# Layer 0's value transposes, sample outputs and last gates, layer 1's query norm rounds and tile copies put in other places

## The chip, the cores and the metric

The kernel runs on one core of a Trainium2 chip. The metric is the device time of one execution in microseconds (us). Five engines work side by side and meet at semaphores: TensorE (PE, with its weight loads as PEld), VectorE (DVE), ScalarE (ACT), GpSimd (POOL) and SyncE (SP); the last two issue most of the DMAs.

## What is computed

Two layers of a hybrid decoder, for a prompt of 512 tokens and for 8 samples of one token each, with the same weights. Both go through the same matmuls as 520 columns.

```python
# layer 0: gated linear attention (4 heads) and retention (4 heads), both recurrent
h  = rms_norm(x, norm_g) * (1.0 + scale) + shift          # scale, shift, gate: silu(c) @ w_ada + b_ada
qa, ka, va, ra, ga, qb, kb, vb, gb = split_cols(h @ w_in, EVEN_SIZES)
o_inter   = q_decayed @ state;  o_intra = scores @ v      # by chunks of 64 tokens
new_state = exp(b_last) * state + k_dec.T @ v             # also for each of the 8 samples
o = rms_norm(o, head_norm_g) * silu(g)
x = x + gate * (concat(oa, ob) @ w_out)
# layer 1: stick-breaking attention (8 heads, q and k normed) and a chunked spatial gate (8 groups)
qc, kc, vc, gc, ud, vd, gd = split_cols(h @ w_in, ODD_SIZES)
log_beta = log_sigmoid(z);  log_rest = where(mask, log_sigmoid(-z), 0)
weight   = exp(log_beta + cumsum_from_right(log_rest) - log_rest);  oc = weight @ v
# the samples attend to 2048 cached keys and values, 16 pages of 128 through a page table
od = gelu(ud) * (tril(w_s) @ rms_norm(gelu(vd)) + b_s)
x = x + gate * (concat(oc * silu(gc), od * silu(gd)) @ w_out)
```

## The kernel before

Activations lie with features on partitions (16 chunks of 128) and the 520 tokens along the free axis. fp32 products are made of two parts: each weight tile (1024 columns of `raw`) is split by ScalarE into `w_hi` (`hi`) and by VectorE into the rest `w_lo` (`lo`), and TensorE multiplies hi*hi, hi*lo and lo*hi. One such tile half is a **unit**: 8 chunks of 6 matmuls, 48 in all; two units fill an output tile in one of two PSUM pairs `pt`, which an engine then copies ("evac") to a buffer `G[...]`. `w_hi` and `w_lo` have two places each, so the split of the unit after next can start only when the unit at hand is done.

The phases follow one another: modulation vectors (`ada0`), the gate's low rank (`ra`), layer 0 (`l0`, 8 heads: 4 GLA, 4 retention), its output projection (`out0`), layer 1's queries and gate inputs (`l1a`, 4 rounds of 8 units), layer 1's heads (`l1b`, 8 heads of 10 units) and `out1`.

Around the units each engine runs the same hand-written order of **steps**. Every phase has a generator on every engine (`mix`), and `go_on(mix)` after a unit runs the next step. In a head of `l0` the units are numbered 0 to 27; 12 of them are weight tiles (u = 2, 3, 8, 9, 12, 13, 16, 17, 22, 23, 26, 27) and the others short matmuls for the modulation of later layers. Steps run after each tile unit and after u = 7 and 21. The function `passed` first plays the second half of the previous head (`rest0`, at u = 2 to 16) and then the first half of this head (`first0`, six steps at u = 17, 21, 22, 23, 26, 27). The last head of layer 0 uses `last_passed`, which also plays four steps of its own `rest0` (`own`) inside and after its last units; the others are played among the first units of `out0`.

`first0` before: PE step 2 (u=21) the decay sums (GLA) or the rotation swap (retention), once key and query are evacuated; step 4 (u=23) ten transposes of the values into M[0] to M[2] (`v_t`), after `qk`; step 5 (u=26) key transposes and scores (`sc`); step 6 (u=27) the first four key-value products (`kv`). VectorE copies the samples' values (`srow0`) from M[0], GpSimd sends them to DRAM and back as a broadcast (`vb_in`), and VectorE, after its first four state steps (`state_steps(i, 0)`), adds them to the eight sample states (eight instructions on one line, semaphore `st_step`). `rest0` before: PE step 1 (u=2) the sample outputs (`os`) and the other four `kv`; step 2 (u=3) the prompt's outputs (`o`).

In `l1a`, ScalarE squares a pair of query tiles at step Q_AT, TensorE sums them over partitions with a matmul by ones at Q_AT+1, and VectorE applies the norm at Q_AT+2. A round of `l1a` has nine steps: one before its first unit and one after each of its 8 units; steps 8 and 9, and 17 and 18, follow each other with no unit between.

Of the kernel before, what the change touches and what calls it, by code (L numbers as in the profile page):

```python
# [12 lines left out]
P = 128  # L13
D = 2048
KC = D // P
T = 512
# [48 lines left out]

Q_AT, V_AT = [4, 8, 13, 17], [22, 26, 31, 35]
L1A_STEPS = 36
# [56 lines left out]
def build(nc, a, o, cst):  # L124
    ctx = ExitStack()
    with ctx:
# [391 lines left out]
        def last_passed(rest, first, own):  # L518

            yield  # L520
            for n in range(8):
                if n != 2:
                    go_on(rest)
                yield
            for n in range(6):
                go_on(first)
                yield
            for n in range(4):
                go_on(own)
                yield  # L530

        def passed(rest, first):
# [12 lines left out]
        def _(pe):  # L545
# [143 lines left out]
            def first0(i, gla):  # L689
                yield  # L690
                pe.wait_ge(s("evac"), i * 6 + (T_L0 + 4))
                if isinstance(i, int) and i == 0:
                    pe.wait_ge(s("la_copied"), 2)
                    pe.wait_ge(s("const_in"), 16 * NCONST)
                else:
                    pe.wait_ge(s("mixed"), i * 2)
                if gla:
                    pe.wait_ge(s("lah"), i + 1)
# [9 lines left out]
                yield  # L708
                yield
                pe.wait_ge(s("qk"), i + 1)  # L710
                for t in range(NT):
                    for d in range(2):
                        tr(M[1 + t // 2][:, 256 * (t % 2) + P * d:256 * (t % 2) + P * d + P],
                           G[d][:, P * t:P * t + P])
                tr(M[0][0:NB, 0:P], G[0][:, T:N])
                tr(M[0][0:NB, P:2 * P], G[1][:, T:N]).then_inc(s("v_t"), 1)
                yield

                pe.wait_ge(s("srow0"), i + 1)
                for t in range(NT):  # L720
                    tr(M[0][:, P * t:P * t + P], G[3][:, P * t:P * t + P])
                pe.wait_ge(s("vtok"), i + 1)
                for t in range(NT):
# [18 lines left out]

            def rest0(i):
                pe.wait_ge(s("st_step"), i * 8 + 8)
                pe.wait_ge(s("sct"), i + 1)
# [3 lines left out]
                last.then_inc(s("os"), 1)  # L749
                key_values(i, 1)  # L750
                yield
                pe.wait_ge(s("s_step"), i * 8 + 8)
# [51 lines left out]
            def l1a_mix():  # L804
                for n in range(L1A_STEPS):
                    for r in range(4):
                        if n == Q_AT[r] + 1:
                            pe.wait_ge(s("q_sq"), r + 1)
                            for t in range(2):
                                mm(M[t], ones[:, :], tmp[t][:, 0:T])  # L810
                                last = mm(M[2][:, 8 * t:8 * t + 8], ones[:, :], tmp[t][:, T:N])
                            last.then_inc(s("q_ss"), 1)
                    if n == Q_AT[3] + 4:
                        pe.wait_ge(s("q_col"), 1)
                        tr(M[1][0:64, 0:P], qcol).then_inc(s("q_t"), 1)
# [149 lines left out]
        def _(act):  # L965
# [13 lines left out]

            def walk(name, i, order, mix=None, ahead=(0, 1), fine=()):  # L980

                go_on(mix)
                split = split_ahead(order, ahead)
                for u in range(2 * len(order)):
                    if u in fine:
                        go_on(mix)
                    if u in split:
                        hi(name, i, split[u])
                    if goes_on(name, order, u):
                        go_on(mix)  # L990
# [75 lines left out]
            def first0(i, gla):  # L1066
                if gla:
                    f(lah, la[:, :, bass.ds(i * P, P)], ACT.Copy).then_inc(s("lah"), 1)
                yield
                if gla:  # L1070
# [6 lines left out]
                yield  # L1077
                act.wait_ge(s("v_t"), i + 1)
                f(vtok[:, 0:2, :], M[1].rearrange("p (t d) -> p t d", t=2), ACT.Copy)
                f(vtok[:, 2:4, :], M[2].rearrange("p (t d) -> p t d", t=2), ACT.Copy).then_inc(s("vtok"), 1)  # L1080
                yield
# [105 lines left out]
            def l1a_mix():  # L1187
                for n in range(L1A_STEPS):
                    for r in range(4):
                        if n == Q_AT[r]:  # L1190
                            act.wait_ge(s("evac"), T_L1A + 2 * r + 2)
                            f(pair_a, pair(r), ACT.Square).then_inc(s("q_sq"), 1)
                        if n == Q_AT[r] + 1:
                            act.wait_ge(s("q_ss"), r + 1)
# [6 lines left out]
                        value_gate(r, n - V_AT[r])  # L1201
                    if n == Q_AT[3] + 4:
                        act.wait_ge(s("q_t"), 1)
# [71 lines left out]
            def l1b(i, odd):  # L1275
                mix = mix1(i, odd)
                walk("l1b", i, L1B_ORDER, mix)
                finish(mix)

            l1b(0, 0)  # L1280
            step.straight()
# [47 lines left out]
        def _(dve):  # L1329
# [27 lines left out]
            def walk(name, i, order, evac=None, par0=0, group=None, mods=(), mix=None, ahead=(0, 1), late=None, fine=()):  # L1357
# [11 lines left out]
                for u in range(2 * len(order)):  # L1369
# [7 lines left out]
                    if order[u // 2] is TILE and u % 2 == 1:  # L1377
                        if t not in late:
                            read_out(t, u)
# [137 lines left out]

            def first0(i, gla):
                yield
                yield  # L1520
# [5 lines left out]
                else:  # L1526
# [13 lines left out]
                yield  # L1540
                dve.wait_ge(s("v_t"), i + 1)
                copy(srow0, M[0][0:NB, 0:256]).then_inc(s("srow0"), 1)
                yield
# [3 lines left out]
                    .then_inc(s("sct"), 1)  # L1547
                dve.wait_ge(s("st_in"), i * 16 + 16)
                step(tt(st, st, small[:, 24:32].unsqueeze(2).to_broadcast([P, NB, 256]), ALU.mult))
                yield  # L1550
                state_steps(i, 0)
                dve.wait_ge(s("vb_in"), 16 * 2 * HEADS + 32 if isinstance(i, int) and i == 2 * HEADS - 1
                            else i * 16 + 16)
                for b in range(NB):
                    stt(st[:, b, :], values(i, b), G[3][:, T + b:T + b + 1], st[:, b, :], ALU.mult, ALU.add)\  # L1555
                        .then_inc(s("st_step"), 1)
                yield

# [18 lines left out]
            def rest0(i):  # L1577
# [178 lines left out]
            def l1a_mix():  # L1756
                for n in range(L1A_STEPS):
                    for r in range(4):
                        if n == Q_AT[r] + 2:
                            dve.wait_ge(s("q_rs"), r + 1)  # L1760
# [4 lines left out]
                        value_gate(r, n - V_AT[r])  # L1765
                    if n == Q_AT[3] + 2:
                        copy(qcol.rearrange("p (b h) -> p h b", b=NB), wide[:, 0:HC, T:N]).then_inc(s("q_col"), 1)
# [380 lines left out]
```

## Time and profile before

| what | us |
|---|---|
| median of 3 runs (2292.97 to 2308.41) | 2301.32 |
| the profiled execution | 2311.7 |
| its span, first to last instruction | 2310.2 |
| mean granted TensorE clock, of full speed | 0.956 |
| `ada0` and `ra`, 0 to 162 | 162 |
| `l0`, 162 to about 954 | 792 |
| `out0` and norm, to about 1185 | 231 |
| `l1a` and `l1b`, to about 2084 | 899 |
| `out1`, to the end | 226 |

The stages are read from the chain and the timeline. "Waits" are an engine's idle time before an instruction, put down to what released it. The granted clock is given in shares of full speed: 1.00 is 2.4 GHz and 0.50 is 1.2 GHz, values between are means over a stretch.

### The profile page before, as it was taken

How to read it: one execution, taken by the hardware profiler on the slowest of the kernel's cores; microseconds unless marked ns; L12 is line 12 of the kernel's file. 1: busy time of each engine (PE TensorE's matmuls, PEld its weight loads, DVE VectorE, ACT ScalarE, POOL GpSimd, SP SyncE). 2: the span in 40 equal slices, each digit the busy share in tenths (PEclk: the TensorE clock that was granted, in tenths of full speed). 3: DMA queues.
4: the chain of work that ended last, by engine and by line, in shares of the span. 5: the costliest groups of instructions: out<-in, count | busy, mean ns of one | idle time of the engine just before them, and what ended most of it. 6: DMA issues, size and time to landing. Idle time of an engine off the chain costs nothing.

```text
span 2310.2 us, 45308 instructions
## 1 busy us (share of the span) xinstructions
PE 2146.0 (93%) x16847; PEld 1888.8 (82%) x16847; DVE 1179.9 (51%) x3657; ACT 587.0 (25%) x733; POOL 201.9 (9%) x319
## 2 busy tenths in 40 slices
PE   6889999999999999799979997999999899999997
PEld 2268888888888878699968897888788788888997
DVE  1533434434454454644462377677677677745332
ACT  1322212121221212322232232233223132324221
POOL 0000101101010110100000001111101101100011
PEclk8789999999999999899979998999999999999999
DMA  9876656466665656333332256887877877853441
GB/s 316 299 235 193 206 171 193 157 200 200 183 189 179 188 166 201 103 115 114 109 138 73 84 165 225 289 279 262 294 255 256 279 245 265 285 174 97 135 128 62
DMA packets 401526, 444.99 MB, mean 193 GB/s; under 512 B 17268, under 2 KB 307406, under 8 KB 399807
## 3 DMA queue, kind: packets, MB, share of 16 engines
q1 hardware_dynamic: 359270, 311.99, 43.9%
q0 software_dynamic: 32288, 122.12, 15.4%
q10 hardware_dynamic: 9810, 8.73, 1.1%
q8 instruction: 103, 1.69, 0.3%
q14 instruction: 55, 0.45, 0.1%
HBM read 416.18 MB, written 26.61 MB: 192 GB/s over the span
## 4 chain that ended last, share of the span: by engine, by line
PE 68%; DVE 15%; DMA 6%; issue 5%; ACT 4%; DVEq 0%; SPq 0%; ACTq 0%; POOLq 0%; POOL 0%
PE pt L547 54%; PE m L547 12%; DVE arena L1727 4%; DMA arena<-in_cache_k 4%; ACT w_hi L969 2%; ACT arena L969 2%; PE m L551 2%; DVE w_lo L1341 1%; DMA raw<-in_e_w_ada 1%; DVE arena L1555 1%; DMA arena<-in_o_k_norm_g 1%; DVE arena L1573 1%; PE pt L551 1%; DVE arena L1515 1%; DVE arena L1891 1%
## 5 line engine op out<-in xcount | busy, mean ns | idle before, releaser
L547 PE MATMUL pt<-act_hi,w_hi 128*128 128x260 f32 x4384 | 918.2, 291 | 42.2 <-DVE w_lo L1341 13.3
L547 PE MATMUL pt<-act_hi,w_lo 128*128 128x260 f32 x4384 | 894.7, 286 | 0.0
L547 PE MATMUL pt<-act_lo,w_hi 128*128 128x260 f32 x4384 | 894.4, 286 | 0.0
L547 PEld LDWEIGHTS pt<-act_hi,w_hi 128*128 128x128 f32 x4384 | 690.1, 193 | 107.0 <-issue 91.7
L1341 DVE TENSOR_TENSOR w_lo<-raw,w_hi 128x1024 fp32r<-128x1024 f32 x274 | 335.3, 1224 | 845.4 <-ACT w_hi L969 845.1
L547 PEld LDWEIGHTS pt<-act_lo,w_hi 128*128 128x128 f32 x4384 | 689.9, 192 | 0.0
L547 PEld LDWEIGHTS pt<-act_hi,w_lo 128*128 128x128 f32 x4384 | 688.5, 192 | 0.0
L969 ACT ACTIVATE w_hi<-raw 128x1024 fp32r<-128x1024 f32 x274 | 289.8, 1058 | 1159.9 <-PE pt L547 1143.0
L1727 DVE CUSTOM_DVE_ANT_0 arena<-arena 128x128 f32<-128x128 f32 x1024 | 224.7, 287 | 60.6 <-DMA arena<-in_cache_k 60.3
L969 ACT ACTIVATE arena<-arena 128x1040 f32<-128x1040 f32 (+8 forms) x191 | 158.1, 837 | 230.5 <-DVE arena L1827 83.0
L547 PE MATMUL m<-raw,cond 128*9 128x512 f32 x768 | 133.8, 663 | 16.4 <-DMA raw<-in_e_w_ada 14.1
L547 PE MATMUL m<-arena 128*128 128x256 f32 (+6 forms) x704 | 128.0, 412 | 21.0 <-DVE arena L1555 20.2
L547 PEld LDWEIGHTS m<-arena 128*128 128x128 f32 (+4 forms) x704 | 79.2, 175 | 60.2 <-DVE arena L1555 21.9
L1976 POOL DMA_DIRECT2D arena<-in_cache_k x128 | 68.0, 531 | 624.7 <-DVE arena L1727 310.6
L547 PEld LDWEIGHTS m<-raw,cond 128*9 128x9 f32 x768 | 17.1, 91 | 81.5 <-DMA raw<-in_e_w_ada 42.9
L551 PE MATMUL m<-c_ident,arena 128*128 128x128 f32 (+2 forms) x403 | 58.3, 276 | 26.0 <-DMA c_fold<-const_fold 8.8
L547 PEld LDWEIGHTS m<-arena,ones 128*128 128x128 f32 (+1 forms) x236 | 43.6, 204 | 43.1 <-issue 19.0
L547 PE MATMUL m<-arena,ones 128*128 128x512 f32 (+3 forms) x236 | 65.5, 392 | 14.4 <-ACT arena L969 8.4
L969 ACT ACTIVATE arena<-m 128x512 f32<-128x512 f32 (+2 forms) x93 | 49.9, 573 | 96.1 <-PE m L547 73.8
L551 PEld LDWEIGHTS m<-c_ident,arena 128*128 128x128 f32 (+2 forms) x403 | 45.0, 143 | 28.6 <-DMA c_fold<-const_fold 8.8
L547 PE MATMUL m<-arena,mod 128*8 128x256 f32 x1024 | 67.2, 380 | 0.0
L2047 POOL TENSOR_SCALAR arena<-arena 128x256 f32<-128x256 f32 x56 | 53.3, 952 | 135.6 <-DVE arena L1566 77.6
(169 smaller groups left out, 1147.3 us busy)
## 6 DMA issues: line engine op xcount, KB each, us to landing
arena<-in_cache_k POOLq DMA_DIRECT2D x128, 512.0 KB, 5.2
arena<-in_cache_v SPq DMA_DIRECT2D x128, 512.0 KB, 5.4
raw<-in_o_w_in SPq DMA_DIRECT2D x112, 512.0 KB, 6.2
raw<-in_e_w_in SPq DMA_DIRECT2D x98, 512.0 KB, 4.6
raw<-in_e_w_ada SPq DMA_DIRECT2D x96, 512.0 KB, 5.8
raw<-in_o_w_ada SPq DMA_DIRECT2D x96, 512.0 KB, 5.2
raw<-in_e_w_out SPq DMA_DIRECT2D x32, 512.0 KB, 3.9
raw<-in_o_w_out SPq DMA_DIRECT2D x32, 512.0 KB, 4.8
```

Source lines behind the costliest of these rows:

```text
L547: return pe.matmul(out, lhsT, rhs, start=start, stop=stop, skip_group_check=True)
L551: return pe.transpose(out, x, ident[0:k, 0:k])
L969: return act.activation(out, x, fn, **kw)
L1341: tt(w_lo[:, b, :], raw[:, sl, :], w_hi[:, b, :].bitcast(F32), ALU.subtract)\
L1515: return ts_(d, x, SCALE, None, ALU.mult) if to == 2 else copy(d, x)
L1555: stt(st[:, b, :], values(i, b), G[3][:, T + b:T + b + 1], st[:, b, :], ALU.mult, ALU.add)\
L1573: stt(S[:, n % 2, :], S[:, (n - 1) % 2, :], small[:, at + 2:at + 3], tmp[4][:, 0:256], ALU.mult, ALU.add).then_inc(s("s_step"), 1)
L1727: last = dve.tensor_tensor_reduce(kpage, kpage, qb[:, P * h:P * h + P], 1.0, 0.0, ALU.mult, ALU.add, to[:, 8 * p + h:8 * p + h + 1])
L1891: tt(z, z, m012[:, 0:SB_ALL], ALU.subtract).then_inc(s("lw"), 1)
L1976: pool.dma_start(pages[:, key_slot(p), :], ck[bass.ds(page, 1)].rearrange("n s d -> (n s) d"))\
L2047: pool.tensor_scalar(carry[:, n, :], S[:, (n - 1) % 2, :], small[:, 6 * (n // 2) + n % 2:6 * (n // 2) + n % 2 + 1], None, ALU.mult).then_i ...
```

## The change

- Layer 0, `first0`: the value transposes and their two copies (`vtok` on ScalarE, `srow0` on VectorE) go from step 4 (u=23) to step 1 (u=17). The decay sums or the swap at u=21 wait for both copies. The scaling of the sample states goes a step forward, to u=23, and the eight sample updates go from behind the first state steps (u=27) to u=26.
- Layer 0, `rest0`: `os` goes from u=2 to u=3, in front of `o`; at u=2 only the four `kv` remain. VectorE takes all six squares in one step.
- Last head: only three own steps are played within layer 0; the fourth (clamp, output norm and sigmoid of the gates) comes after the first four chunks of `out0`.
- `l1a`: the sum, the norm and the query column follow a list Q_SUM = [5, 10, 14, 19].
- `l1b`: ScalarE copies the output tiles out of `pt`, after its split for the next unit; VectorE no longer does.

```diff
-Q_AT, V_AT = [4, 8, 13, 17], [22, 26, 31, 35]
+Q_AT, Q_SUM, V_AT = [4, 8, 13, 17], [5, 10, 14, 19], [22, 26, 31, 35]
@@ last_passed
-            for n in range(4):
+            for n in range(3):
                 go_on(own)
                 yield
+            yield
@@ tensor, first0
-                yield
-                pe.wait_ge(s("evac"), i * 6 + (T_L0 + 4))
+                pe.wait_ge(s("evac"), i * 6 + (T_L0 + 2))
                 ...
+                for t in range(NT):
+                    for d in range(2):
+                        tr(M[1 + t // 2][:, 256 * (t % 2) + P * d:256 * (t % 2) + P * d + P],
+                           G[d][:, P * t:P * t + P])
+                tr(M[0][0:NB, 0:P], G[0][:, T:N])
+                tr(M[0][0:NB, P:2 * P], G[1][:, T:N]).then_inc(s("v_t"), 1)
+                yield
+                pe.wait_ge(s("evac"), i * 6 + (T_L0 + 4))
+                pe.wait_ge(s("vtok"), i + 1)
+                pe.wait_ge(s("srow0"), i + 1)
                 ...
                 yield
                 yield
+                yield
+
                 pe.wait_ge(s("qk"), i + 1)
                 ...
-                tr(M[0][0:NB, P:2 * P], G[1][:, T:N]).then_inc(s("v_t"), 1)
-                yield
@@ tensor, rest0
+                key_values(i, 1)
+                yield
                 pe.wait_ge(s("st_step"), i * 8 + 8)
                 ...
                 last.then_inc(s("os"), 1)
-                key_values(i, 1)
-                yield
                 pe.wait_ge(s("s_step"), i * 8 + 8)
@@ tensor and scalar, l1a_mix (vector likewise, with + 1)
-                        if n == Q_AT[r] + 1:
+                        if n == Q_SUM[r]:
@@ scalar, walk
                         hi(name, i, split[u])
+                    if evac is not None and u % 2:
+                        act.wait_ge(s("pe_tile"), tile_no(name, i, u) + 1)
+                        evac(u // 2, pt[(par0 + u // 2) % 2][:, :, 0:HALF]).then_inc(s("evac"), 1)
@@ vector, first0
+                dve.wait_ge(s("v_t"), i + 1)
+                copy(srow0, M[0][0:NB, 0:256]).then_inc(s("srow0"), 1)
                 yield
                 ...
-                dve.wait_ge(s("v_t"), i + 1)
-                copy(srow0, M[0][0:NB, 0:256]).then_inc(s("srow0"), 1)
+                dve.wait_ge(s("st_in"), i * 16 + 16)
+                step(tt(st, st, small[:, 24:32].unsqueeze(2).to_broadcast([P, NB, 256]), ALU.mult))
                 ...
-                yield
-                state_steps(i, 0)
                 dve.wait_ge(s("vb_in"), 16 * 2 * HEADS + 32 if isinstance(i, int) and i == 2 * HEADS - 1
                             else i * 16 + 16)
                 for b in range(NB):
                     stt(st[:, b, :], values(i, b), G[3][:, T + b:T + b + 1], st[:, b, :], ALU.mult, ALU.add)\
                         .then_inc(s("st_step"), 1)
+                yield
+                state_steps(i, 0)
                 yield
@@ vector, rest0
-                dve.wait_ge(s("o_a"), i * 2 + 1)
-                squares((4, 5))
                 yield
                 dve.wait_ge(s("o_a"), i * 2 + 2)
-                squares(range(4)).then_inc(s("o_ss"), 1)
+                squares(range(6)).then_inc(s("o_ss"), 1)
@@ vector, l1b
-                walk("l1b", i, L1B_ORDER, lambda k, x: copy(halves(G[L1B_TO[k]]), x), (T_L1B + odd) % 2, mix=mix)
+                walk("l1b", i, L1B_ORDER, None, mix=mix)
```

## Rows read from the trace of the kernel before

**Rows 1.** The page, busy time of TensorE, share of the span, instructions.
```profile
PE 2146.0 (93%) x16847; PEld 1888.8 (82%) x16847; DVE 1179.9 (51%) x3657; ACT 587.0 (25%) x733; POOL 201.9 (9%) x319
```

**Rows 2.** TensorE's waits, whole span: for whom, us in total, times, longest.
```profile
PE m L547 <- DVE arena L1555: 20.2, 8, 5.1
...
PE m L547 <- DVE arena L1515: 9.8, 8, 1.3
...
PE m L547 <- ACT arena L969: 8.4, 2, 4.2
...
PE m L547 <- DVE arena L1781: 7.5, 8, 3.9
...
PE m L551 <- DVE arena L1539: 6.1, 3, 2.1
```

**Rows 3.** Timeline of TensorE, heads' starts: start, us, instruction, [idle before <-releaser].
```profile
353.05 2.71 PE L547 MATMUL m<-arena 128*32 128x256 f32 x24 [2.06 <-DVE arena L1555]
...
853.20 2.13 PE L547 MATMUL m<-arena 128*32 128x256 f32 x24 [2.19 <-DVE arena L1555]
```

**Rows 4.** The chain of waits: start, us, the unit behind each of them.
```profile
355.75 6.93 PE pt L547 x48
...
855.34 5.95 PE pt L547 x48
```

**Rows 5.** Windows of TensorE behind a head's start: stretch, busy, clock, DMA share.
```profile
355.70:362.60 6.90, 6.90 (x51) 0.84 0.25 89
```

**Rows 6.** Timeline of VectorE, the end of one GLA head, start of the next.
```profile
338.05 2.28 DVE L1549 TENSOR_TENSOR arena<-arena 128x2048 f32<-128x2048 f32 x1
...
349.51 3.48 DVE L1555 SCALAR_TENSOR_TENSOR arena<-wide,arena 128x256 f32<-128x256 f32 x8
352.91 1.22 DVE L1341 TENSOR_TENSOR w_lo<-raw,w_hi 128x1024 fp32r<-128x1024 f32 x1
355.80 0.48 DVE L1568 TENSOR_SCALAR arena<-m,arena 128x256 f32<-128x256 f32 x1 [1.67 <-PE m L547]
...
359.80 0.48 DVE L1573 SCALAR_TENSOR_TENSOR arena<-arena 128x256 f32<-128x256 f32 x1
```

**Rows 7.** Timelines of ScalarE, TensorE and GpSimd, the same place.
```profile
351.02 1.06 ACT L969 ACTIVATE w_hi<-raw 128x1024 fp32r<-128x1024 f32 x1 [6.91 <-PE pt L547]
...
342.95 1.14 PE L547 MATMUL m<-arena 64*128 64x256 f32 x8
...
367.67 0.90 POOL L2026 DMA_DIRECT2D arena<-in_state_gla  x1 [5.11 <-DMA out_gla_sample<-arena]
```

**Rows 8.** Timelines of TensorE, VectorE and ScalarE, the decay sums and value copies.
```profile
311.93 0.48 PE L547 MATMUL m<-c_cum_mid,arena 128*128 128x128 f32 x2 [1.26 <-DVE arena L1515]
...
329.95 0.40 DVE L1542 COPY arena<-m 8x256 f32<-8x256 f32 x1
...
309.84 0.61 ACT L969 ACTIVATE arena<-arena 128x512 f32 x1
...
328.20 1.09 ACT L969 ACTIVATE arena<-m 128x512 f32<-128x512 f32 x2
```

**Rows 9.** Timeline of TensorE, the value transposes of a retention head.
```profile
625.19 1.31 PE L551 MATMUL m<-c_ident,arena 128*128 128x128 f32 x10 [2.07 <-DVE arena L1539]
```

**Rows 10.** Timelines of TensorE and ScalarE, last head of layer 0 into `out0`.
```profile
936.01 3.94 PE L547 MATMUL m<-arena 128*32 128x256 f32 x24 [5.07 <-DVE arena L1555]
...
962.75 0.77 PE L547 MATMUL pt<-act_hi,w_hi 128*128 128x260 f32 x2 [8.54 <-DVE act_lo L1426]
...
958.07 3.27 ACT L969 ACTIVATE arena<-arena 128x1040 f32<-128x1040 f32 x3 [2.71 <-DVE arena L1596]
```

**Rows 11.** Timeline of TensorE, first and second query sums in `l1a`.
```profile
1209.80 2.22 PE L547 MATMUL m<-arena,ones 128*128 128x512 f32 x8
...
1233.60 4.43 PE L547 MATMUL m<-arena,ones 128*128 128x512 f32 x8 [4.18 <-ACT arena L969]
```

**Rows 12.** Groups by line and form: the copies of `l1b`, count | busy, mean ns.
```profile
L1906 DVE COPY arena<-pt 128x520 f32<-128x520 f32 x40 | 27.8, 696 | 17.8 <-PE pt L547 17.8
```

**Rows 13.** Timeline of TensorE, the longest wait of `l1b` for the masks.
```profile
1815.39 2.07 PE L547 MATMUL m<-arena,c_from_key 128*128 128x512 f32 x2 [3.90 <-DVE arena L1781]
```

More of the change, by code:

```diff
@@ L709, in first0 @@
                 yield
+                yield
                 pe.wait_ge(s("qk"), i + 1)
                 for t in range(NT):
[L712 to L715, printed above, removed]
-                tr(M[0][0:NB, P:2 * P], G[1][:, T:N]).then_inc(s("v_t"), 1)
-                yield
-                pe.wait_ge(s("srow0"), i + 1)
-                for t in range(NT):
                     tr(M[0][:, P * t:P * t + P], G[3][:, P * t:P * t + P])
-                pe.wait_ge(s("vtok"), i + 1)
                 for t in range(NT):
@@ L812, in l1a_mix @@
                             last.then_inc(s("q_ss"), 1)
-                    if n == Q_AT[3] + 4:
+                    if n == Q_SUM[3] + 2:
                         pe.wait_ge(s("q_col"), 1)
@@ L978, in hi, with walk @@
                 f(w_hi[:, tile_no(name, i if isinstance(i, int) else 0, u) % 2, :], raw[:, sl, :], ACT.Copy).then_inc(s("split_hi"), 1)
-            def walk(name, i, order, mix=None, ahead=(0, 1), fine=()):
+            def walk(name, i, order, mix=None, ahead=(0, 1), fine=(), evac=None, par0=0):
                 go_on(mix)
@@ L1068, in first0 @@
                     f(lah, la[:, :, bass.ds(i * P, P)], ACT.Copy).then_inc(s("lah"), 1)
+                act.wait_ge(s("v_t"), i + 1)
+                f(vtok[:, 0:2, :], M[1].rearrange("p (t d) -> p t d", t=2), ACT.Copy)
+                f(vtok[:, 2:4, :], M[2].rearrange("p (t d) -> p t d", t=2), ACT.Copy).then_inc(s("vtok"), 1)
                 yield
@@ L1077, in first0 @@
                 yield
-                act.wait_ge(s("v_t"), i + 1)
-                f(vtok[:, 0:2, :], M[1].rearrange("p (t d) -> p t d", t=2), ACT.Copy)
-                f(vtok[:, 2:4, :], M[2].rearrange("p (t d) -> p t d", t=2), ACT.Copy).then_inc(s("vtok"), 1)
                 yield
@@ L1192, in l1a_mix @@
                             f(pair_a, pair(r), ACT.Square).then_inc(s("q_sq"), 1)
-                        if n == Q_AT[r] + 1:
+                        if n == Q_SUM[r]:
                             act.wait_ge(s("q_ss"), r + 1)
@@ L1201, in l1a_mix @@
                         value_gate(r, n - V_AT[r])
-                    if n == Q_AT[3] + 4:
+                    if n == Q_SUM[3] + 2:
                         act.wait_ge(s("q_t"), 1)
@@ L1276, in l1b @@
                 mix = mix1(i, odd)
-                walk("l1b", i, L1B_ORDER, mix)
+                walk("l1b", i, L1B_ORDER, mix,
+                     evac=lambda k, x: f(G[L1B_TO[k]].rearrange("p (a n) -> p a n", a=2), x, ACT.Copy),
+                     par0=(T_L1B + odd) % 2)
                 finish(mix)
+            act.wait_ge(s("evac"), T_L1B)
             l1b(0, 0)
@@ L1377, in walk @@
                     if order[u // 2] is TILE and u % 2 == 1:
-                        if t not in late:
+                        if t not in late and evac is not None:
                             read_out(t, u)
@@ L1547, in first0 @@
                     .then_inc(s("sct"), 1)
-                dve.wait_ge(s("st_in"), i * 16 + 16)
-                step(tt(st, st, small[:, 24:32].unsqueeze(2).to_broadcast([P, NB, 256]), ALU.mult))
-                yield
-                state_steps(i, 0)
                 dve.wait_ge(s("vb_in"), 16 * 2 * HEADS + 32 if isinstance(i, int) and i == 2 * HEADS - 1
@@ L1556, in first0 @@
                         .then_inc(s("st_step"), 1)
+                yield
+                state_steps(i, 0)
                 yield
@@ L1758, in l1a_mix @@
                     for r in range(4):
-                        if n == Q_AT[r] + 2:
+                        if n == Q_SUM[r] + 1:
                             dve.wait_ge(s("q_rs"), r + 1)
@@ L1765, in l1a_mix @@
                         value_gate(r, n - V_AT[r])
-                    if n == Q_AT[3] + 2:
+                    if n == Q_SUM[3] + 1:
                         copy(qcol.rearrange("p (b h) -> p h b", b=NB), wide[:, 0:HC, T:N]).then_inc(s("q_col"), 1)
```

## The prediction

> **What bounds the kernel now.** The page's busy times come first: TensorE is busy for 93% of the span, VectorE for 51% and ScalarE for 25% [rows 1]. So the time can only fall by what TensorE idles, and by what it does slowly. The list of TensorE's waits says where it idles [rows 2]. The reader is to see five items that belong to places the diff touches: 20.2 us for line 1555 (the eight sample updates), 9.8 us for line 1515 (the evacuation in front of the decay sums or the swap), 6.1 us for line 1539 (`qk`, in front of the value transposes), 8.4 us for ScalarE in two waits (the query norm) and 7.5 us for line 1781 (the masks of layer 1). Together they are 52.0 us. Then the timeline around one wait of each sort, with the chain and the windows, shows what follows it. After the idle 2.06 us at a head's start the 24 matmuls take 2.71 us and the next unit 6.93 us, where another head has 2.13 and 5.95 us after the same wait [rows 3, 4]. In that slow unit's stretch the granted clock is 0.84 [rows 5], a mean of stretches at 2.4 and at 1.2 GHz; the engine had idled just before it. So most waits are paid twice: in idle time and in matmuls at 1.2 GHz.
>
> **Head starts of layer 0 (line 1555).** Seven of the eight waits stand at the start of a head, 20.2 - 5.1 = 15.1 us in all [rows 2]. TensorE's step at u=2 waits for the sample updates, which VectorE did last, from 349.51 to 353.0 [rows 6]. After the change this step holds only the four `kv`, which need the first four state steps. These end where the updates begin now, at 349.51, and TensorE comes at 353.05 - 2.06 = 350.99, so the wait is gone with 1.5 us to spare. The updates (3.48 us) go to u=26: VectorE can start them at 338.05, where the scaling (2.28 us, moved to u=23) stands now, and ends at 341.5, before TensorE's `kv` at 342.95 [rows 6, 7]; what is queued behind them, the next `w_lo` and the state steps, is not delayed. `os` now stands in front of `o` at u=3. Is `o` late? VectorE's second state steps take 355.80 to 360.28, 4.5 us [rows 6]. New start: the `w_hi` split ends at 352.08, `w_lo` 1.22 us later, so steps from 353.3 to 357.8. TensorE comes at 350.99 + 1.14 (`kv`) + 5.95 (unit) = 358.1, and does `os` first (2.13 - 1.14 = 1.0). So `o` finds its states with 1.3 us to spare [rows 3, 4, 6, 7]. The POOL queue waits for `os` before it loads the next sample states; now that wait ends some 7 us later, at about 359, but the load is let go by the landing of the store at 367.67 [rows 7], so nothing moves. Gain: 15.1 us of idle. The slow matmuls go with it: (2.71 + 6.93) - (2.13 + 5.95) = 1.56 us, in six of the seven (the seventh is the one at 853.20), 9.4 us. Bounds of this clock part: 0 and 9.4; I take 9.4, since where the engine does not idle in a head its clock is 1.00. The Trainium skill (TensorE: Matmul & The Clock Gate, Part 1) says that which matmuls run at half rate varies from run to run of one program. The trace agrees as far as it goes, one of seven equal waits has no fall; by the page alone the term would be anything from 0 to 9.4.
>
> **Value transposes.** They leave u=23, where three of the four retention heads wait for `qk`: 6.1 us gone [rows 2, 9]; at u=26 `qk` is a unit old. At u=17 they take 1.31 us [rows 9], straight after the unit, when VectorE and ScalarE are still at split and evacuation. The decay sums or the swap at u=21 wait 1.26 us now [rows 8]. TensorE comes 1.31 us later, so the evacuation is over; new behind it is the copy `srow0`, 0.40 us [rows 8]. Left: 1.26 + 0.40 - 1.31 = 0.35 us. ScalarE: the `lah` copy ends at 310.45, the two copies need 1.09 more, 311.5; TensorE comes at 311.93 - 1.26 + 1.31 = 311.98, so they are no wait. Gain: 9.8 - 8 x 0.35 = 7.0 us. The DMAs: the round trip through DRAM now starts at about 312 and is used at 338; today it starts behind 329.95 and is used without a wait at 349.51, so 19.6 us are enough and 26 are there [rows 6, 8].
>
> **Last head.** The 5.07 us wait [rows 10] is for the updates again; they leave VectorE's line in front of it, 3.4 us of it go, 1.7 stay (in this head the steps come at half units). Into `out0` TensorE idles 8.54 us. ScalarE's first activation chunks stand behind the sigmoid, 3.27 us, which itself waits 2.71 us for VectorE's clamp [rows 10]. After the change four chunks go first: TensorE starts between 3.27 and 5.98 us earlier, but chunks 5 and on stand behind the same sigmoid and may be waited for. Bounds 0 and 6.0; I take 3.3. Sum: 6.7 us.
>
> **Query norm.** Sums 2 and 4 stand directly behind the unit whose tile is squared, so TensorE waits for evacuation and square: 4.18 us, and then the eight matmuls take 4.43 us instead of 2.22 [rows 11]. A unit later the square is long done. Gain 2 x (4.18 + 4.43 - 2.22) = 12.8 us. ScalarE and VectorE have the same spacing as in round 1, which runs without a wait; rounds of keys start at step 23 and keep their place.
>
> **Copies of layer 1.** VectorE loses 40 copies of 696 ns, 27.8 us [rows 12]; ScalarE gains 40, at about 0.55 us each by the two in 1.09 us [rows 8], 22 us. ScalarE is a quarter busy, and the copy stands behind the split and before the step, which at those places waits for others. TensorE needs the tile only a whole tile later. On TensorE's path lies only the chain to the masks: 7.5 us in eight waits, the longest 3.90 [rows 2, 13], each shorter by at most 0.7 us. Bounds: a loss of 40 x 0.55 = 22 us if every copy lay on the path, a gain of 5.6 us; nearest to the row of waits is a gain of 3 us.
>
> **Sum.** 15.1 + 9.4 + 6.1 + 7.0 + 6.7 + 12.8 + 3 = 60.1 us. The profiled execution took 2311.7 us (span 2310.2 and 1.5 around it), so 2251.6. It lies 10.4 us over the median shown; taking the sum from the median gives 2241.
>
> **The rivals.** (a) The idle time goes but the clock falls somewhere else as often: without 9.4 and 2 x 2.21 the sum is 46.3, 2255 us. For it: one of seven waits without a fall, so idle and fall are not tied one to one. Against: at 1.00 in the long stretches. The skill's sentence above would fit this case. (b) A new wait takes the place at u=3: `o` has 1.3 us to spare and a state step more or a later split uses it up. With 2 us in seven heads and the slow clock kept, 14 + 9.4 are lost, sum 36.7, 2265 us. (c) The other side: VectorE now waits for the broadcast values at u=26, in front of the `w_lo` of a coming unit. If it came late, units would stall in all eight heads. It decides when the values land later than the 26 us by 60.1 / 8 = 7.5 us plus the 5.95 us of a unit that a split may be late: over 39 us for what takes under 19.6 today. Ten us beyond the slack, in eight heads, give 2241 + 80 = 2321 us. (d) It does not do what it says: TensorE's stalls are replaced in the same step by others (`srow0`, sigmoid) and only the query rounds count: 2289 us.
>
> **How the numbers follow.** Forecast 0.60, (a) 0.20, (b) 0.12, (d) 0.05, (c) 0.03. The low end takes the upper bounds: last head 5 more, layer 1 5 more (a late page as in [rows 13] costs some us more or less per head), and 15 for the spread of the runs shown: 2216. The high end lies just above (b): 2268. A measurement of this kernel tells about 1% (23 us) from no change: faster by more is the forecast, (a) and (b), 0.92; within 1% is (d), 0.05; slower (c), 0.03.
>
> **What would show it.** Right: in the waits of TensorE no line of sample updates but a wait of some 2 us in the last head; no `qk` wait; the waits in front of decay sums and swap near 0.35 us; the 24-matmul groups split, units behind them 5.8 to 6.0 us; four query sums of 2.2 us; VectorE's busy time down by 28 us and ScalarE's up by 22. Wrong: TensorE waiting in layer 0 for line 1573 or GpSimd's carries, a slice of low clock without idle before it, or waits for `w_lo` in layer 1 beyond today's.

## The result, and the profile after

| | before | after |
|---|---|---|
| median of four runs | 2300.84 us (2292.97 to 2308.41) | 2237.47 us (2233.98 to 2239.81) |
| ratio of the two, 95% interval | | 0.9724 (0.9689 to 0.9759) |
| profiled execution (span) | 2311.7 us (2310.2) | 2237.85 us (2236.3) |
| mean granted clock | 0.956 | 0.974 |

The kernel is faster by 63.4 us, or 2.8%; the forecast was 2241. Between the two profiled executions the difference is 73.9 us, since the profiled execution of before, which is not among the four runs, lies 10.9 us over their median, and that of after, which is one of its four, 0.4 us over theirs. The section on why takes up that gap of 10.5 us. In the code of after the matmul helper is line 548 (547 before), the transposes are 552, the evacuation of layer 0's tiles is 1523 and `srow0` is 1528, the updates are 1561, the state steps 1576 and 1581, and the masks 1787.

The page of after: first the busy times, to be held against [rows 1], then the chain by engine.

```profile
PE 2116.0 (95%) x16847; PEld 1868.0 (84%) x16847; DVE 1156.1 (52%) x3617; ACT 605.5 (27%) x773; POOL 200.5 (9%) x319
...
PE 82%; DVE 9%; ACT 3%; DMA 3%; issue 3%; SPq 0%; DVEq 0%; ACTq 0%; POOLq 0%
```

TensorE issues as many matmuls as before, but is busy for 30.0 us less: the same work, at the higher of the two clock levels more of the time. The other 43.9 us of the 73.9 are idle time of TensorE that is gone. VectorE is busy for 23.8 us less, ScalarE for 18.5 us more (28 and 22 were forecast); the 40 copies themselves went as read, 27.8 us off VectorE and 23.5 onto ScalarE, and the rest of the two differences was not followed.

TensorE's waits in after, whole span (whom it waits for, us in total, times, longest), to be held against [rows 2]:

```profile
PE m L548 <- DVE arena L1528: 4.3, 8, 0.8
...
PE m L548 <- DVE arena L1787: 1.9, 8, 0.3
...
PE m L548 <- DVE arena L1581: 1.5, 1, 1.5
```

Of the five items of [rows 2], 52.0 us, 7.7 us are left. No line of the updates is left, none of `qk`, none of ScalarE's query squares. Line 1528, `srow0`, is the new wait in front of decay sums and swap; line 1581, a state step, is the one wait of the last head.

The timeline of TensorE at the start of a GLA head (start, us, instruction). It answers [rows 3]:

```profile
340.81 1.13 PE L548 MATMUL m<-arena 64*128 64x256 f32 x8
...
347.84 4.87 PE L548 MATMUL m<-arena 128*32 128x256 f32 x38
```

The 24 matmuls behind a wait of 2.06 us have become two groups without a wait: `kv` alone, eight matmuls in 1.13 us, and a unit later the sample outputs together with `o`. The unit between them, on the chain of waits, to be held against [rows 4]:

```profile
341.94 5.97 PE pt L548 x48
```

It takes 5.97 us, as the faster of the two of before did. The next row is of before again, a window of TensorE (stretch, length, busy time and count, granted clock, DMA share, GB/s) over the units behind the decay sums of a GLA head:

```profile
404.00:418.00 14.00, 12.74 (x95) 0.88 0.62 184
```

Its clock is 0.88: the granted clock goes down to the lower level for a part of this stretch and comes back. Such an event is called a fall below, and this one the prediction had not looked at. Of after, whole heads, a GLA head first and a retention head second, with all engines (busy times of TensorE, weight loads, VectorE, ScalarE, GpSimd; then clock, DMA share, GB/s):

```profile
254.80:347.90 93.10, 92.64 (x769) 82.47 (x772) 41.56 (x70) 21.44 (x28) 10.07 (x12) 1.00 0.63 194
628.10:721.70 93.60, 93.10 (x761) 81.92 (x762) 45.44 (x77) 19.77 (x23) 10.57 (x13) 1.00 0.64 199
```

The clock is 1.00 through both, and TensorE idles 0.46 and 0.50 us in them. A GLA head of before took 99.0 us and the longest of three retention heads 101.7, both at 0.97.

**Where the 73.9 us lie.** The same points of the program in both timelines give:

| stretch | before, us | after, us | gain |
|---|---|---|---|
| up to layer 0 (nothing there is changed) | 166.4 | 164.4 | 2.0 |
| heads, to 13.6 us into the last one's start | 700.3 | 657.5 | 42.8 |
| rest of the last head, start of `out0` | 125.5 | 115.4 | 10.1 |
| `out0` and the norm behind it | 200.2 | 200.2 | 0.0 |
| `l1a`, the query rounds | 121.0 | 107.0 | 14.0 |
| `l1a`, keys and values | 163.9 | 163.8 | 0.1 |
| `l1b` | 601.0 | 596.1 | 4.9 |
| `out1` to the end | 231.9 | 231.9 | 0.0 |

The windows of TensorE over the second row, before and after, show what the 42.8 us are made of (columns as in the window above: length, busy time and count, clock, DMA share, GB/s):

```profile
166.40:866.70 700.30, 668.92 (x5323) 0.97 0.60 187
...
164.40:821.90 657.50, 652.23 (x5322) 1.00 0.64 199
```

The same matmuls take 16.7 us less, at a clock of 1.00 in place of 0.97, and 26.1 us of idle time are gone. Ahead of layer 0, where nothing is changed, the clock was 0.85 in the one execution and 0.90 in the other.

### The profile page after: what moved, and what is told of

Same layout as the page of the kernel before. It is cut to its first block, busy times and chain, and to the rows that moved or that the text cites. A ratio compares the mean times of both kernels' runs of the same rounds, so it can differ in the third digit from the quotient of the medians.

```text
span 2236.3 us, 45304 instructions
## 1 busy us (share of the span) xinstructions
PE 2116.0 (95%) x16847; PEld 1868.0 (84%) x16847; DVE 1156.1 (52%) x3617; ACT 605.5 (27%) x773; POOL 200.5 (9%) x319
## 4 chain that ended last, share of the span: by engine, by line
PE 82%; DVE 9%; ACT 3%; DMA 3%; issue 3%; SPq 0%; DVEq 0%; ACTq 0%; POOLq 0%
PE pt L548 65%; PE m L548 15%; DVE arena L1733 2%; PE m L552 2%; ACT w_hi L971 2%; ACT arena L971 1%; DMA raw<-in_e_w_ada 1%; DVE w_lo L1349 1%; DMA arena<-in_o_k_norm_g 1%; PE pt L552 1%; DVE arena L1897 1%; DVE arena L1787 0%; DMA arena<-in_cache_k 0%; DVE arena L1468 0%; DVE act_lo L1429 0%
## 5 line engine op out<-in xcount | busy, mean ns | idle before, releaser
L548 PE MATMUL m<-arena 128*128 128x256 f32 (+6 forms) x704 | 121.7, 383 | 2.3 <-DVE arena L1581 1.5
L548 PEld LDWEIGHTS m<-raw,cond 128*9 128x9 f32 x768 | 16.6, 90 | 81.5 <-DMA raw<-in_e_w_ada 43.2
L548 PE MATMUL m<-arena,ones 128*128 128x512 f32 (+3 forms) x236 | 60.5, 369 | 5.9 <-DVE arena L1662 5.9
```

The lines of the kernel that those rows point to most:

```text
L548: return pe.matmul(out, lhsT, rhs, start=start, stop=stop, skip_group_check=True)
```

## The experiments

Each time stands beside the median of the kernel before on the same chip; a gain is the difference of the two medians, and its bounds are those of the ratio's 95% interval times that median. The ratio on record is not the quotient of the two medians, so the two can differ by some us; where that bears on a choice, both are given. The first six runs put the heads' change or one part of the whole into the kernel before. The last four start from the kernel after, which was not run beside them, so a difference of medians to it is less sure than one to before.

### Heads of layer 0 alone

The kernel before with the value transposes at u=17, the sample outputs at u=3, scaling and updates moved; the last gates, the query rounds and the copies of `l1b` stay.

```diff
 def rest0(i):                      # TensorE
+    key_values(i, 1)
+    yield
     pe.wait_ge(s("st_step"), i * 8 + 8)
     ...
-    key_values(i, 1)
-    yield
```

> The kernel before with the change of layer 0's heads alone (values at u=17, updates at u=26, sample outputs at u=3). Theory, idle time and the slow matmuls behind it both go: 15.1 + 9.4 + 6.1 + 7.0 + 3.4 (last head) = 41 us less. Rival, the falls of the clock stay: 31.6 us less. A head of GLA should go from 99.0 to about 94 us, one of retention from 101.3 to about 94.5.

Measured: 2255.5 against 2298.51 us, 43.0 us less (35.6 to 48.7). A GLA head takes 93.1 us and a retention head 93.6, a little under what was expected. TensorE's waits are those of after in the heads, and the eight waits in front of decay sums and swap come to 4.2 us:

```profile
PE m L547 <- DVE arena L1521: 4.2, 8, 0.7
...
PE m L547 <- DVE arena L1574: 1.5, 1, 1.5
```

43 us are two thirds of the gain of the whole. 31.6, the value if the falls stay, lies below the interval: the slow matmuls went with the idle time.

### Sample outputs a step later, alone

```diff
 def rest0(i):                      # VectorE
-    dve.wait_ge(s("o_a"), i * 2 + 1)
-    squares((4, 5))
     yield
     dve.wait_ge(s("o_a"), i * 2 + 2)
-    squares(range(4)).then_inc(s("o_ss"), 1)
+    squares(range(6)).then_inc(s("o_ss"), 1)
```

TensorE as in the diff above; ScalarE's copy of the sample outputs goes a step later too. Scaling, updates and value transposes stay where they were.

> The kernel before with the sample outputs a step later alone; the eight updates stay behind the first state steps, the values at u=23. Theory, moving the updates adds nothing to it in heads 1 to 7: seven waits of 2.15 us and six slow groups of 1.56 go, 24.5 us less, as in the whole change; VectorE ends the second state steps 0.9 us later than with the updates moved, still 0.4 us ahead of TensorE. Rival: the updates in front of the second state steps make the prompt's outputs wait at u=3, by 1 us or more in seven heads, and the gain falls below 15 us.

Measured: 2277.22 against 2298.51 us, 21.3 us less (14.9 to 26.2). That holds the expected 24.5, and its low end touches the rival's 15, so the trace has to tell. The starts of heads 1 to 7 have no wait left, though the updates still stand last on VectorE. So it is the consumer's move that removes the wait; the updates' move is not needed for it, except in the last head. There TensorE waits 1.45 us for a state step, as in after (1.51), and then 2.14 us for a carry of GpSimd, which after does not have:

```profile
903.89 1.14 PE L547 MATMUL m<-arena 64*128 64x256 f32 x8 [1.45 <-DVE arena L1573]
...
912.21 5.23 PE L547 MATMUL m<-arena 128*128 128x256 f32 x22 [2.14 <-POOL arena L2045]
```

The second wait is rival (b), for one head. The untouched waits of line 1515 (9.8 us) and 1539 (6.1 us) stand in its list as in [rows 2], and behind two of the four decay sums and two of the three `qk` waits the clock still falls. In windows of TensorE, a GLA head with such a fall and one without:

```profile
252.60:348.00 95.40, 94.14 (x768) 0.98 0.61 189
...
443.40:537.30 93.90, 92.64 (x768) 1.00 0.62 192
```

The two differ by 1.5 us, with the same idle time in them (1.26 us each).

### Value transposes at u=17, alone

```diff
 def first0(i, gla):                # TensorE
+    for t in range(NT):
+        for d in range(2):
+            tr(M[1 + t // 2][:, 256 * (t % 2) + P * d:256 * (t % 2) + P * d + P],
+               G[d][:, P * t:P * t + P])
+    tr(M[0][0:NB, 0:P], G[0][:, T:N])
+    tr(M[0][0:NB, P:2 * P], G[1][:, T:N]).then_inc(s("v_t"), 1)
     yield
     pe.wait_ge(s("evac"), i * 6 + (T_L0 + 4))
+    pe.wait_ge(s("vtok"), i + 1)
+    pe.wait_ge(s("srow0"), i + 1)
```

These ten transposes stood behind `qk`, at u=23. The copies `vtok` and `srow0` move to the same step.

> The kernel before with the value transposes and their two copies at u=17 alone; updates and sample outputs stay. Theory: the three qk waits (6.1 us) go and the waits in front of decay sums and swap fall from 1.23 to 0.35 us, 7.0 us, together 13.1 us less; the waits for the updates stay at 2.2 us. If the falls of the clock behind the decay sums of the four GLA heads go too, 1.2 us each, 18 us less.

Measured: 2280.39 against 2299.44 us, 19.0 us less (4.4 to 25.3): wide, five runs from 2271.17 to 2295.99, and by the ratio (0.9935) 15.0. So it bears out a gain but doesn't choose between 13.1 and 18. The list of waits shows what went: `qk` (line 1539 before) is gone, the waits of decay sums and swap are 4.2 us (0.53 each, 0.35 were expected), and the 20.2 us for the updates stay.

```profile
PE m L547 <- DVE arena L1556: 20.2, 8, 5.1
...
PE m L547 <- DVE arena L1521: 4.2, 8, 0.7
```

The timeline of its head starts shows that one and the same idle is paid twice in one head and not in the next:

```profile
251.08 3.58 PE L547 MATMUL m<-arena 128*32 128x256 f32 x24 [2.19 <-DVE arena L1556]
...
347.63 2.14 PE L547 MATMUL m<-arena 128*32 128x256 f32 x24 [2.06 <-DVE arena L1556]
...
442.79 3.68 PE L547 MATMUL m<-arena 128*32 128x256 f32 x24 [2.19 <-DVE arena L1556]
```

### Query rounds alone

```diff
-Q_AT, V_AT = [4, 8, 13, 17], [22, 26, 31, 35]
+Q_AT, Q_SUM, V_AT = [4, 8, 13, 17], [5, 10, 14, 19], [22, 26, 31, 35]
```

> The kernel before with the query sums at 5, 10, 14, 19 alone. Theory, paid twice: 2 x (4.18 + 4.43 - 2.22) = 12.8 us less, four query sums of 2.2 us. Rival, the fall of the clock only moves: 8.4 us less.

Measured: 2281.02 against 2298.51 us, 17.5 us less (10.3 to 21.8). The waits for ScalarE are gone and the second sum, 4.43 us behind 4.18 us of idle in [rows 11], is

```profile
1218.80 2.22 PE L547 MATMUL m<-arena,ones 128*128 128x512 f32 x8
```

8.4 us, the idle time without the slow matmuls, lies outside the interval; the expected 12.8 lie in it.

### ScalarE's copies of layer 1's tiles, alone

```diff
-walk("l1b", i, L1B_ORDER, lambda k, x: copy(halves(G[L1B_TO[k]]), x), (T_L1B + odd) % 2, mix=mix)
+walk("l1b", i, L1B_ORDER, None, mix=mix)      # VectorE; ScalarE copies in its own walk
```

> The kernel before with ScalarE's copies of layer 1's tiles alone. Theory: the masks' waits shorten by up to 0.7 us each, 3 us less (0 to 5.6). Rival, the copies delay ScalarE's splits: up to 22 us more, waits of TensorE for w_lo in layer 1.

Measured: 2293.72 against 2298.51 us, 4.8 us less (1.4 to 8.7; twelve runs against seventeen; 3 were expected). TensorE's wait for the masks is 1.9 us in eight:

```profile
PE m L547 <- DVE arena L1787: 1.9, 8, 0.3
```

### Last gates behind four chunks, alone

```diff
-            for n in range(4):
+            for n in range(3):
                 go_on(own)
                 yield
+            yield
```

> The kernel before with the last head's gates behind four chunks of the output projection alone. Theory: TensorE's 8.5 us wait shortens by 4 to 5 us, a new wait of 1 to 2 us stands in front of the fifth chunk: 3.3 us less (0 to 6). Rival: the sigmoid is only moved, no gain at all.

Measured: 2295.62 against 2299.44 us, 3.8 us less, with an interval that holds zero (-0.9 to 6.7), so the rival, no gain, isn't excluded by the times. In the timeline of TensorE 8.54 us of [rows 10] are now two waits:

```profile
949.88 0.48 PE L548 MATMUL pt<-act_hi,w_hi 128*128 128x260 f32 x2 [3.77 <-DVE act_lo L1427]
...
956.89 0.48 PE L548 MATMUL pt<-act_hi,w_hi 128*128 128x260 f32 x2 [2.38 <-DVE act_lo L1427]
```

6.15 us in place of 8.54: the first chunk comes 4.8 us sooner, and half of that is given back at the fifth chunk, behind the sigmoid. From the first chunk to the loop of `out0` TensorE then needs 32.3 us where the kernel before needed 29.4, so 1.9 us of the 4.8 are left. The kernel with the heads alone and the kernel after differ by the same step at this place, and there it is worth 2.0 us, from the last head's swap to that loop. Both are less than the 3.3 expected.

### An idle put back at seven head starts

The kernel after, in which TensorE at u=2 of heads 1 to 7 waits for the low split of unit 8, which it needs only later. Nothing else changes.

```diff
-def rest0(i):
+def rest0(i, late=None):           # late: the split of u=8
+    if late is not None:
+        pe.wait_ge(s("split_lo"), late + 1)
```

> The kernel after with one wait more on TensorE in heads 1 to 7: at u=2, in front of the four key-value products, it waits for the w_lo of the unit after next, about 2.3 us. No work is added. Theory, such idle time is paid twice: 7 x 2.3 = 16 us of idle plus six or seven times 1.5 us of slow matmuls, 25 to 27 us more. Rival, the falls of the clock do not hang on it: 16 us more.

Measured: 2259.36 us, 21.9 us over the median of after (2237.47); ratio to before 0.9836 (0.9808 to 0.9863), after's being 0.9724, which makes 25.8. Its profiled execution has a span of 2260.2 us, 23.9 us over after's. The idle is

```profile
PE m L548 <- DVE w_lo L1351: 17.8, 7, 2.6
```

so 6.1 us of the 23.9 are not idle time. The windows of TensorE behind two of the seven, from `kv` to the end of the unit:

```profile
347.30:354.40 7.10, 7.07 (x60) 1.00 0.25 74
443.10:450.40 7.30, 7.30 (x47) 0.77 0.23 72
```

After idles of 2.5 to 2.6 us, four of the seven windows have 0.76 to 0.78 and three have 1.00. Four falls of about 1.5 us are 6.0: 17.8 + 6.0 = 23.8, all but 0.1 us of what was measured. Both expected values missed: 16 us leaves out the falls, 25 to 27 has six or seven of them where the trace has four. This settles the mechanism of the clock term: the idle alone, put back into heads 1 to 7, in which TensorE otherwise never waits more than 0.6 us, brings slow matmuls back, but not behind every idle.

### A shorter idle at the same places

The same with the high split, which ScalarE writes earlier.

```diff
-        pe.wait_ge(s("split_lo"), late + 1)
+        pe.wait_ge(s("split_hi"), late + 1)
```

> The same as the run before with the wait for the w_hi alone, about 1.1 us in heads 1 to 7. Idle alone 8 us more. Theory: an idle time of 1.1 us lowers the clock in some heads only, as the 1.26 us wait did in the four GLA heads and not in the retention heads: 8 to 13 us more. Rival: every idle time is paid twice, 16 us more.

Measured: 2247.71 us, 10.2 us over after (span 9.9 over); ratio to before 0.9796 (0.9766 to 0.9826), which makes 16.6 us over after. By the times, then, neither the 8 us of idle alone, nor the 8 to 13 expected, nor the rival's 16 is excluded, and the reading rests on the trace. The idle is 8.6 us, and a whole head with such a wait in it keeps its clock:

```profile
PE m L548 <- ACT w_hi L973: 8.6, 7, 1.2
...
350.80:445.20 94.40, 92.70 (x769) 1.00 0.62 190
```

No window of the seven is below 1.00: in this execution none of the idles is paid twice, and the expected falls in some heads did not come. The heads as a whole are 8.6 us longer than after's. The other 1.3 us of the 9.9 lie at the start of `out0`, which the edit doesn't touch. There the wait in front of the fifth chunk is 2.36 us where after has 1.47, and from the first chunk to the loop TensorE needs 32.3 us, not 30.8:

```profile
922.44 0.77 PE L548 MATMUL pt<-act_hi,w_hi 128*128 128x260 f32 x2 [2.36 <-DVE act_lo L1436]
```

### After with the copies back on VectorE

```diff
-walk("l1b", i, L1B_ORDER, None, mix=mix)
+walk("l1b", i, L1B_ORDER, lambda k, x: copy(halves(G[L1B_TO[k]]), x), (T_L1B + odd) % 2, mix=mix)
```

> The kernel after with layer 1's tile copies back on VectorE. Theory: 3 us more than the kernel after (0 to 5.6), the masks' waits of layer 1 back at 0.8 us and more. Rival, the copies' place does not matter: the same time.

Measured: 2238.94 us, ratio to before 0.9746 (0.9718 to 0.9773) where after has 0.9724 (0.9689 to 0.9759). The intervals overlap, so the time alone doesn't tell 3 us from nothing. TensorE's wait for the masks is back:

```profile
PE m L548 <- DVE arena L1781: 8.3, 8, 3.7
```

All seven kernels whose copies are VectorE's have 3.2 to 8.3 us there (before 7.5), and all five with ScalarE's have 1.9 or 2.0. By these waits the copies are worth 1.2 to 6.4 us, depending on the execution.

### After with the gates behind eight chunks

Tried as a version that might beat the kernel after: if half of the gain at the first chunk is lost at the fifth, put the sigmoid behind all of them.

```diff
-for c in range(4):
+for c in range(8):
     take(c)
 go_on(rest)
-for c in range(4, 8):
-    take(c)
```

This is ScalarE's side; VectorE takes eight chunks in front of the step as well.

> The kernel after with the gates' step of the last head behind eight chunks of the output projection instead of four, on ScalarE and VectorE. Theory: the wait of 1.5 us in front of the fifth chunk goes, chunks 5 to 8 follow at VectorE's pace of 0.61 us, and the step is hidden: 1 to 3 us less than the kernel after. Rival: chunks 15 and 16 need the gated output, which now comes later: a new wait in front of them, no gain.

Measured: 2234.42 us, ratio 0.9722 (0.9693 to 0.9751): not told apart from after. In the timeline the second wait is gone and the stretch from the first chunk to the loop of `out0` is 29.1 us instead of 30.8:

```profile
907.20 0.77 PE L548 MATMUL pt<-act_hi,w_hi 128*128 128x260 f32 x2 [3.77 <-DVE act_lo L1432]
```

That is a gain of 1.8 us by the timeline, within the 1 to 3 expected, which the times neither bear out nor exclude.

## Why the prediction was right, and which of its terms were off

The parts add: 43.0 for the heads, 17.5, 4.8 and 3.8 come to 69.1 us, and the whole's 63.4 us has an interval of 55.5 to 71.6. So it is not that the stalls only changed place (rival d), nor does the broadcast of the values come late (rival c): the updates start behind `sct` at 327.95 without a wait.

```profile
327.95 3.25 DVE L1561 SCALAR_TENSOR_TENSOR arena<-wide,arena 128x256 f32<-128x256 f32 x8
...
347.25 0.48 DVE L1581 SCALAR_TENSOR_TENSOR arena<-arena 128x256 f32<-128x256 f32 x1
```

The second row is the last state step of a head; it ends at 347.73, and TensorE comes to the sample outputs at 347.84 and to `o` about 1 us later. So `o` has some 1.1 us to spare where 1.3 were foreseen: rival (b) lost narrowly.

Term by term, forecast beside what the two profiled executions show:

| term | forecast | shown | |
|---|---|---|---|
| idle at head starts | 15.1 | 15.1 | gone whole |
| `qk` | 6.1 | 6.1 | gone whole |
| decay sums and swap | 7.0 | 5.5 | 0.46 to 0.56 us left in each, 0.76 in the first, not 0.35 |
| slow matmuls in the heads | 9.4 | 16.7 | TensorE's busy time in the heads; see below |
| last head and `out0` | 6.7 | 9.5 | 10.1 less the 0.6 of its swap, which stands above |
| query rounds | 12.8 | 14.0 | |
| copies of `l1b` | 3 | 4.9 | forecast between 0 and 5.6 |
| before layer 0 | | 2.0 | not the change's |
| sum | 60.1 | 73.8 | |

**Decay sums and swap** (mis-sized, 1.5 us too much): the step was right, the evacuation and then `srow0` are in the way, but the sum counted only the instructions' own times. TensorE waits for `srow0`, which VectorE starts at 304.00 and ends at 304.40, and comes to its matmuls 0.1 us later:

```profile
304.50 0.46 PE L548 MATMUL m<-c_cum_mid,arena 128*128 128x128 f32 x2 [0.46 <-DVE arena L1528]
...
584.29 2.30 PE L548 MATMUL m<-arena,c_swap 128*128 128x512 f32 x8 [0.56 <-DVE arena L1528]
```

**Last head and `out0`** (2.8 us too little). The wait of 5.07 us became 1.51, as forecast (1.7), and the 8.54 us became 3.77 and 1.47. That is 3.3 us less idle, the value taken between bounds of 0 and 6, but by luck: the step itself gained 1.9 to 2.0 us, as the experiment on the last gates shows, since the matmuls behind the first chunk take longer. What the sum left out is that the matmuls behind the 5.07 us were slow too. Of TensorE, to be held against [rows 10]:

```profile
886.97 1.13 PE L548 MATMUL m<-arena 64*128 64x256 f32 x8 [1.51 <-DVE arena L1581]
...
906.50 0.77 PE L548 MATMUL pt<-act_hi,w_hi 128*128 128x260 f32 x2 [3.77 <-DVE act_lo L1434]
...
913.51 0.48 PE L548 MATMUL pt<-act_hi,w_hi 128*128 128x260 f32 x2 [1.47 <-DVE act_lo L1434]
```

The clock term was worked out for seven head starts and not for the eighth, whose 24 matmuls took 3.94 us in [rows 10] where they take 2.13 at full clock; that gives 1.8 us, and what was slow in the units behind it and at the start of `out0` comes on top.

**Slow matmuls in the heads.** This is the term that was right for the wrong reason. The prediction read six falls of the clock at head starts from one execution and took them as a property of the kernel. The profiled executions of the kernels with only the query rounds, the copies or the last gates changed run the very same eight heads, with the same waits to within 0.2 us. Their timelines hold other numbers of falls. A fall shows as a 24-matmul group over 2.13 us, as 31.0 us instead of 29.45 from a GLA head's decay sums to its `kv`, or as 17.7 instead of 16.1 from a retention head's value transposes to its `kv`:

| kernel whose trace it is | falls at 7 head starts | between them, behind decay sums or `qk` | first head start to last, us | without 1.56 us for each fall |
|---|---|---|---|---|
| before | 6 | 4 | 681.9 | 666.3 |
| copies alone | 6 | 3 | 679.9 | 665.9 |
| last gates alone | 4 | 2 | 675.8 | 666.4 |
| query rounds alone | 3 | 0 | 670.4 | 665.8 |

(For before, one more fall stands ahead of the first head start: its first decay sums.) One number explains the four lengths to 0.7 us: each fall costs 1.56 us, as worked out in the prediction from [rows 3, 4], and only how many there are changes from one execution to another. The profiled execution of before, with its eleven falls (17 us; 16.7 by its busy time), lies 10.9 us over the median of the four runs, which fits a count that changes with the execution. It is not all that changes: the four runs of before are 15 us apart and those of after 6, but those of heads alone are 10 us apart too and the six with the copies back on VectorE 12, and the profiled executions of these two show no fall in the heads. In after the seven stretches from a head start to the next head's decay sums or swap are 56.8 us long, one 57.3, and those from GLA decay sums to `kv` 28.3 us, all four: no fall in the heads at all.

So an estimate for the medians is this. The idle that went in the heads, 26.1 us, and the gains of the other three places in the profiled pair, 10.1, 14.0 and 4.9, sum to 55.1 us; 63.4 - 55.1 leaves 8.3 us for the heads' slow matmuls in a typical execution, some five falls. With the interval of the 63.4 it could be none or ten. In the profiled pair the same account is 55.1 + 16.7 + 2.0 = 73.8. The forecast of 9.4 counted six falls at head starts and missed those behind the decay sums and `qk` (five in the profiled execution). Against a typical execution the two errors nearly cancel, and that is luck; against the profiled one they don't.

The Trainium skill (TensorE: Matmul & The Clock Gate, Part 1), which the prediction weighed, says that one kernel has 6, 11 or 14 slow matmuls from run to run. It says so of a kernel's start. Here the falls within the heads vary in the same way: 3, 6, 9 and 10 of them behind the same waits. Rival (a) had the falls move elsewhere; in the heads of after there is none.

**Query rounds.** The wait of 4.18 us and the slow group of 4.43 us are gone in both places, and the four sums take 2.22 us each. The stretch is 14.0 us shorter, 1.2 more than forecast. Most of it is slow matmuls behind the slow sums, as the chain of before shows for the 144 matmuls behind the second wait (18.00 us) and a like group without a fall (17.42):

```profile
1212.02 17.42 PE pt L547 x144
...
1295.33 18.00 PE pt L547 x144
```

Over the 816 matmuls of the tiles in this stretch the two chains differ by 0.9 us.

**Copies.** In the groups by line and form, ScalarE's copies (count, busy, mean ns, idle before) are cheaper than VectorE's were in [rows 12], and none is waited for:

```profile
L971 ACT ACTIVATE arena<-pt 128x520 f32<-128x520 f32 x40 | 23.5, 586 | 0.0
```

The gain came out near the upper end of the forecast, and for another reason than the one given. The prediction let each wait for the masks shrink by at most the 0.7 us of a copy. But the wait of 3.90 us of [rows 13] went down to 0.24, and so did every other one of 0.8 us or more. That the sum of the eight went from 7.5 to 1.9 us, just the 5.6 of the upper bound, is chance: with VectorE's copies it is 3.2 to 8.3 us, depending on the trace. Why the long waits vanish isn't shown.

**What stays open.** Why a given idle is followed by a fall and its twin in the next head isn't, the traces don't show. Nor do they show why waits of 1.24 to 1.26 us in front of the decay sums were followed by falls in before, while 1.2 us in front of `kv` never was (none of seven). And why the first chunks of `out0` are faster in some executions than in others, which decides how long the fifth is waited for (1.47 or 2.4 us), has no cause shown.

## What to carry to other kernels

Price an idle of the busiest engine at its length and what the clock does behind it, but take the second from several executions: here each fall cost 1.56 us and the same code had between 3 and 10 of them, so one profile doesn't give the term. Where the bounding engine waits for the last in a row of jobs, move the consumer a step later, past other work that is ready, before moving the producer: this alone gave 21 of the 43 us, and where no later step is left (the last head) the producer's move is what helps. A copy on the busy path of one engine can go to an engine that at this point only waits.

## What the runs showed of the hardware that was not expected

- Seven equal idles of 2.5 to 2.6 us in otherwise dense work: granted clock 0.76 to 0.78 over the 7 us behind four of them, 1.00 behind three. Each fall costs about 1.5 us.
- Seven idles of 1.2 us at the same places: the clock is 1.00 behind all, in the one execution traced. Yet waits of 1.24 to 1.26 us in front of the decay sums were followed by a fall in four GLA heads of four in the trace of before, in two of four with the copies alone and with the sample outputs alone, in one with the last gates alone, and in none with the query rounds alone.
- A wait of 3.77 us was followed by 5.5 us at half clock in after, by the windows of TensorE; behind the same wait of 3.77 us with the last gates alone and with the shorter idle the mean clock of those 5.5 us was 0.69:

```profile
903.00:906.50 3.50, 0.00 (x0) 0.87 0.01 2
906.50:912.00 5.50, 5.50 (x24) 0.50 0.48 143
```

- Twice in each run, at the turn of `l1b`'s loop, TensorE pauses with nothing to wait for that the profile shows, 6.8 to 7.8 us together. No part of the change moved it; in after:

```profile
PE pt L548 <- issue: 7.4, 2, 3.8
```
